# Two token tiles of the last run read the second expert table in order, by matrix products, instead of gathering its rows

## The chip, the core and the metric

The kernel runs on one core of a Trainium2 chip. Five engines have instruction streams of their own: TensorE (PE), VectorE (DVE), ScalarE (ACT), GpSimd (POOL) and SyncE (SP). They meet through semaphores. POOL issues the row gathers, SP most other transfers, and all transfers of the core run on its 16 DMA engines. The metric is the device time of one execution in microseconds (us).

## What is computed

A layer of a streaming encoder for 1024 prompt tokens and 32 sample tokens of width 1024, everything in float32. The attention branches and projections stand first. What matters here is the retrieval of single-neuron experts behind them:

```
sc = einsum("thjd,hjnd->thjn", q, subkeys)      # 8 heads, 2 halves, 128 keys
s1, i1 = top_k(sc[:, :, 0], 16);  s2, i2 = top_k(sc[:, :, 1], 16)
best, sel = top_k(s1 + s2 (all 256 pairs), 16)  # idx = i1 * 128 + i2 of those picked
g  = softmax(best)
ue = take(u, idx);  ve = take(v, idx)           # tables u, v: 16384 rows x 1024
a  = gelu(einsum("thkd,td->thk", ue, h))
y  = x + einsum("thk,thkd->td", g * a, ve)      # then a final rmsnorm
```

Each token thus picks 8 x 16 = 128 rows of `u` and the same 128 rows of `v`, 4 KB each.

## The kernel before

The tokens lie in tiles of 128 (tile 8 holds the 32 sample tokens). They are worked in three runs, (0, 1, 8), (2, 3, 4) and (5, 6, 7), and each run goes through dense stages: inputs, attend, merge, out, score. `ORDER` lists the tiles by place, so places 6, 7 and 8 are tiles 5, 6 and 7, the third run.

The expert work is a second program, woven between the dense stages. It goes in **steps** k = 0 to 1099. Sixteen steps make a group (one head of one tile). A full tile has 128 steps, place 6 begins at step 672, place 7 at 800, place 8 at 928, and the dots end with step 1055. In step k:

- POOL (`pool`) issues the gather of the `u` rows of step k (`gather_u`, 128 rows, 512 KB) and, 40 steps late (`V_LAG`), the gather of `v` rows number k - 40 (`gather_v`). Both pass through the helper `gather`, line 713. The `u` rows have one row for each token's partition, the `v` rows are sorted otherwise: one gather holds 128 picks of a few tokens.
- DVE (`experts_dve`) waits for the `u` rows and forms the dot products of 128 tokens in one instruction (line 2060). In steps 0, 2, 4, 6 and 8 of a group it also ranks the next group's scores (`rank`, `gate`), which gives the indices.
- ACT (`experts_act`) does the exponentials and the gelu, and spreads each pair of groups' weights into the matrix `zw` (`spread`).
- PE (`weigh_rows`, line 2226) takes four `v` gathers at a time, a **quad**: 8 products of 128x32 weights with 512 columns, summed in the PSUM tile `y_sum`.

At a tile's end (`tile_end`) DVE adds the residual row `x1` and normalises (`finish_sum`, `finish_norm`), and ACT stores it. POOL keeps 8 `u` and 10 `v` buffers in flight while dense stages run; 16 steps after the last dense stage's step (735) the memory of those stages is used for 5 and 4 more (`MORE_U`, `MORE_V`, class `Ring`). Step lists are fixed in the code: `plan` sets, by costs written in `ticks`, at which step each dense piece stands, and every engine follows the same weave.

Of the kernel before, what the change touches and what calls it, by code (L numbers as in the profile page):

```python
# [219 lines left out]
PIECES = [sum(64 if t == SAMPLE else 256 for t in ORDER[:at]) for at in range(TILES + 1)]  # L220


class Ring:


    def __init__(self, n, more, at, total):
        free, uses, last = list(range(n)), [0] * (n + more), [None] * (n + more)
        self.slot, self.use, self.prev = [], [], []
        for k in range(total):
            if k == at:  # L230
                free = list(range(n, n + more)) + free
            slot = free.pop(0)
            free.append(slot)
            uses[slot] += 1
            self.slot.append(slot)
            self.use.append(uses[slot])
            self.prev.append(last[slot])
            last[slot] = k
# [11 lines left out]
class Kernel:  # L250
# [8 lines left out]
    def memory(self):  # L259
# [15 lines left out]
        self.ranks = keep("ranks", [P, TOPK])  # L275
# [52 lines left out]
        with ExitStack() as ctx:  # L328
            self.u_rows += [sb(ctx, f"G_u_rows{SLOTS_U + i}", [P, D]) for i in range(MORE_U)]
            self.v_rows += [sb(ctx, f"G_v_rows{SLOTS_V + i}", [P, D]) for i in range(MORE_V)]  # L330
# [140 lines left out]

    def semaphores(self):
# [49 lines left out]
        self.u_in = [sem(f"g_u_in{i}") for i in range(SLOTS_U + MORE_U)]  # L522
        self.v_in = [sem(f"g_v_in{i}") for i in range(SLOTS_V + MORE_V)]
# [4 lines left out]
        self.y_taken, self.squares, self.roots, self.y_ready = (sem(n) for n in ("g_y_taken", "g_squares", "g_roots", "g_y_ready"))  # L528

    def counts(self):  # L530
# [16 lines left out]
        self.last_dense = self.plan()[-1] - PRELUDE + 2 * SLOTS_U  # L547
        self.ring_u = Ring(SLOTS_U, MORE_U, self.last_dense, U_SLOTS)
        self.ring_v = Ring(SLOTS_V, MORE_V, self.last_dense - V_LAG, U_SLOTS)
        self.f_out0 = sums([16 * (1 + sp.sample) * HEADS // 2 for sp in SPANS])  # L550

# [91 lines left out]
    def pool(self, pool):  # L643
# [15 lines left out]
        pool.iota(self.ranks[:, :], pattern=[[1, TOPK]], base=0, channel_multiplier=0,  # L659
# [1310 lines left out]
    def rank(self, dve, m, piece):  # L1970
# [31 lines left out]
        else:  # L2002
# [14 lines left out]
            dve.tensor_reduce(self.key[:, :, :].rearrange("p j k -> p (j k)"), hot[:, :, :], AX, ALU.add)  # L2017
            dve.drain()
            cols = slice(TOPK * (m % 2), TOPK * (m % 2 + 1))
            dve.scalar_tensor_tensor(out=self.idx[m // 2 % 2][:, cols], in0=self.key[:, 0, :], scalar=float(P), in1=self.key[:, 1, :],  # L2020
                                     op0=ALU.mult, op1=ALU.add).then_inc(self.ranked, 1)
            if m % 2:
                dve.drain()
                dve.transpose(self.idxT[m // 2 % 3][:, :], self.idx[m // 2 % 2][:, :]).then_inc(self.idx_turned, 1)
# [7 lines left out]
    def weigh(self, dve, n):  # L2032
        b = n // 2
        cols = slice(TOPK * (n % 2), TOPK * (n % 2 + 1))
        dve.wait_ge(self.gelu_done, n + 1)
        dve.tensor_tensor(self.weights[b % 2][:, cols], self.gelus[n % 2][:, :], self.gates[n % 4][:, :], ALU.mult)
        if n % 2:
            if b >= 2:
                dve.wait_ge(self.z_made, b - 1)
            dve.drain()  # L2040
            dve.transpose(self.wT[b % 2][:, :], self.weights[b % 2][:, :]).then_inc(self.w_turned, 1)

    def experts_dve(self, dve):
# [7 lines left out]
        finish = {tile_end(at) + 2: at for at in range(TILES)}  # L2051
        for k in range(STEPS):
# [22 lines left out]
            if k - 1 in finish:  # L2075
                self.finish_norm(dve, finish[k - 1])
            yield

    def finish_sum(self, dve, t):
        x1 = self.x1  # L2080
        dve.wait_ge(self.weighed, (tile_end(t) + 1 - V_LAG) // 4)
# [7 lines left out]
    def finish_norm(self, dve, t):  # L2089
        if t == 0:  # L2090
            dve.wait_ge(self.g_fin_in, 16)
        dve.wait_ge(self.roots, t + 1)
# [48 lines left out]
    def store_y(self, act, at):  # L2141
        act.wait_ge(self.y_ready, at + 1)
# [8 lines left out]
    def spread(self, act, b):  # L2151

        z, first = self.zw[b % 2], 4 if GROUP[2 * b][1] == SAMPLE else 0
# [11 lines left out]
    def experts_act(self, act):  # L2165
# [10 lines left out]
        finish = {tile_end(at) + 2: at for at in range(TILES)}  # L2176
        h2_at = {TOPK * FIRST[at] - 20: at for at in range(1, TILES)}
        x1_at = {TOPK * FIRST[at] + 58: at for at in range(TILES)}
        for k in range(STEPS):
# [4 lines left out]
            if c == 2 and n % 2 == 0 and 2 <= n <= GROUPS_ALL:  # L2184
                self.spread(act, n // 2 - 1)
# [25 lines left out]
    def weigh_rows(self, pe, quad):  # L2211
        b, i = divmod(quad, QUADS)
        at = GROUP[2 * b][0]
        first, last_of = 2 * b == FIRST[at] and i == 0, 2 * b + 2 == FIRST[at + 1] and i == QUADS - 1
        if i == 0:
            pe.wait_ge(self.z_made, b + 1)
        if first and at:
            pe.wait_ge(self.y_taken, at)
# [9 lines left out]
        last.then_inc(self.weighed, 1)  # L2228

# [6 lines left out]
def build(nc, a, outs):  # L2236
# [6 lines left out]
    with ExitStack() as ctx:  # L2243
# [8 lines left out]
        def _(sp):  # L2252
            k.weave(k.dense(k.inputs_sp, k.memory_sp, k.attend_sp, k.merge_sp, k.out_sp, k.score_sp, sp), idle(sp, STEPS + PRELUDE))

# [77 lines left out]
```

## Time and profile before

| | us |
|---|---|
| median of 3 executions | 4154.73 |
| lowest, highest | 4143.67, 4164.61 |
| span of the profiled execution | 4055.0 |
| median less span | 99.7 |
| PE, DVE, POOL busy | 2755.5, 2362.3, 2392.4 |
| moved by all transfers | 1373.95 MB, of it 1107.43 MB by the gathers' queue |

The span runs from the first to the last instruction; launch and end lie around it. A busy share over the whole span mixes the dense stages with the last quarter, in which only the expert steps are left, so the stages have to be read apart. "Granted clock" is TensorE's clock as a part of 2.4 GHz; the two levels it has are 1.2 and 2.4 GHz, and a value between is a mixture over the stretch. A wait marked "issue" is one in which the engine waited for nothing that the profile shows. A product in float32 leaves two matmul records in the trace.

### The profile page before, as it was taken

To read this page: it belongs to the slowest core of one execution; us is meant where nothing else is said; L and a number is where in the kernel's file an instruction comes from. 1 tells how busy PE (TensorE), PEld (TensorE's weight loads), DVE (VectorE), ACT (ScalarE), POOL (GpSimd) and SP (SyncE) were. 2 spreads that over 40 slices of the span, in tenths; PEclk is the share of its full clock that TensorE was granted. 3 is DMA by queue.
4 is the path that set the end of the run, shared out by engine and by line. 5 is a ranking of instruction groups with operands and counts; after the bars stand their busy time and mean duration, and the time that the engine had idled before them with its cause. 6 is when DMAs were issued, how large, how long until landed. Compare 5 with 4: busy or idle time off the path is not lost.

```text
span 4055.0 us, 39016 instructions
## 1 busy us (share of the span) xinstructions
PE 2755.5 (68%) x12071; PEld 1452.6 (36%) x12071; DVE 2362.3 (58%) x6192; ACT 853.5 (21%) x1884; POOL 2392.4 (59%) x2148
## 2 busy tenths in 40 slices
PE   8989987877789975568787888987453332333334
PEld 5667564534445432234444444443121000000000
DVE  2134356578865556646488886654566666666552
ACT  1235212244421110112144442111010000000000
POOL 1000034667756547756477776654777777777775
PEclk9989988977779987779877778998776665566556
DMA  6443387999999989989999999997999999999998
GB/s 219 124 142 101 139 285 268 389 359 385 390 349 394 386 336 375 395 312 387 356 387 361 385 394 394 381 374 289 368 391 388 381 370 367 385 387 366 382 369 345
DMA packets 540797, 1373.95 MB, mean 339 GB/s; under 512 B 50640, under 2 KB 246800, under 8 KB 540592
## 3 DMA queue, kind: packets, MB, share of 16 engines
q0 software_dynamic: 304128, 1107.43, 71.4%
q1 hardware_dynamic: 195040, 220.24, 16.2%
q10 hardware_dynamic: 41424, 43.80, 3.3%
q8 instruction: 99, 1.62, 0.2%
q14 instruction: 106, 0.87, 0.1%
HBM read 1319.26 MB, written 52.02 MB: 338 GB/s over the span
## 4 chain that ended last, share of the span: by engine, by line
PE 33%; POOL 25%; DMA 13%; DVE 11%; issue 10%; DVEq 3%; ACT 2%; SPq 1%; ACTq 1%; PEldq 0%; POOLq 0%; PEld 0%
POOL G_v_rows L713 13%; POOL G_u_rows L713 12%; PE scores L837 7%; DMA G_v_rows<-in_peer_v,G_idxT 5%; PE scores L1721 5%; PE y_sum L2226 4%; PE scores L1725 3%; DVE G_u_rows L2060 3%; PE scores L1915 3%; PE scores L1503 3%; PE scores L1810 2%; DMA scratch_dkT<-A_dkT 2%; PE scores L1410 2%; PE o L1445 1%; DMA D_w_br<-in_w_br_m 1%
## 5 line engine op out<-in xcount | busy, mean ns | idle before, releaser
L713 POOL DMA_INDIRECT G_u_rows<-in_peer_u,G_idx x1056 | 1199.9, 1136 | 756.7 <-issue 321.8
L2060 DVE CUSTOM_DVE_ANT_0 G_u_rows<-G_u_rows,G_h 128x1024 f32<-128x1024 f32 x1056 | 1274.7, 1221 | 431.2 <-DMA G_u_rows<-in_peer_u,G_idx 408.4
L713 POOL DMA_INDIRECT G_v_rows<-in_peer_v,G_idxT x1056 | 1177.9, 1115 | 486.9 <-issue 312.4
L2226 PE MATMUL y_sum<-G_v_rows,G_zw 128*32 128x512 f32 x4224 | 749.7, 846 | 877.1 <-DMA G_v_rows<-in_peer_v,G_idxT 853.0
L2226 PEld LDWEIGHTS y_sum<-G_v_rows,G_zw 128*32 128x32 f32 x4224 | 148.9, 137 | 1358.5 <-issue 1354.6
L837 PE MATMUL scores<-A_w_in,A_hT 128*128 128x256 f32 (+2 forms) x864 | 221.9, 417 | 22.9 <-DMA A_w_in<-in_w_in 15.5
L668 POOL MEMSET G_zw<- 128x1024 f32 x2 | 1.9, 963 | 395.9 <-SPq L630 395.9
L837 PEld LDWEIGHTS scores<-A_w_in,A_hT 128*128 128x128 f32 x864 | 168.7, 198 | 74.8 <-DMA A_w_in<-in_w_in 16.4
L1721 PE MATMUL scores<-D_hT,D_w_gate 128*128 128x384 f32 x512 | 172.9, 491 | 2.3 <-DMA D_w_br<-in_w_br_m 2.1
L1428 PE MATMUL turn<-ident,C_probs 128*128 128x128 f32 x635 | 133.4, 327 | 49.1 <-ACT C_pT L1536 41.2
L1960 DVE COPY F_sc<-scores 128x256 f32<-128x256 f32 (+1 forms) x72 | 29.3, 422 | 215.2 <-PE scores L1926 215.1
L1523 ACT ACTIVATE C_probs<-C_probs,C_ntop 128x128 f32<-128x128 f32 (+5 forms) x144 | 104.8, 729 | 187.3 <-DVEq L1597 182.2
L2183 ACT ACTIVATE G_gelus<-G_dots 128x16 f32<-128x16 f32 x66 | 14.2, 216 | 602.6 <-DVEq L2064 602.3
L1428 PEld LDWEIGHTS turn<-ident,C_probs 128*128 128x128 f32 x635 | 87.8, 170 | 144.7 <-ACT C_pT L1536 75.0
L837 PE MATMUL scores<-A_hT,A_w_in 128*128 128x384 f32 x384 | 132.4, 499 | 9.7 <-issue 9.7
L1410 PE MATMUL scores<-C_k_diff,C_q_diff 32*128 32x512 f32 (+4 forms) x416 | 108.5, 631 | 44.3 <-DVE C_ntop L1594 36.9
L1915 PE MATMUL scores<-h2T,F_w_q 128*128 128x384 f32 (+1 forms) x384 | 126.7, 489 | 17.1 <-DMA F_skT<-scratch_skT 17.1
L1599 DVE TENSOR_REDUCE C_ntop<-scores 128x1 f32<-128x256 f32 (+8 forms) x108 | 65.9, 610 | 121.3 <-PE scores L1410 120.3
L1536 ACT ACTIVATE C_pT<-turn 128x512 f32<-128x512 f32 (+3 forms) x216 | 102.7, 475 | 135.8 <-PE turn L1428 135.0
L1410 PE MATMUL scores<-C_k_mla,C_q_mla 104*128 104x512 f32 (+4 forms) x208 | 97.8, 588 | 42.3 <-SPq L630 36.3
L1721 PEld LDWEIGHTS scores<-D_hT,D_w_gate 128*128 128x128 f32 x512 | 95.3, 190 | 83.8 <-issue 17.6
L1915 PE MATMUL scores<-h2T,DF_w 128*128 128x384 f32 (+1 forms) x384 | 124.6, 483 | 1.0 <-issue 0.6
(282 smaller groups left out, 3940.7 us busy)
## 6 DMA issues: line engine op xcount, KB each, us to landing
A_w_in<-in_w_in SPq DMA_DIRECT2D x24, 1024.0 KB, 13.3
D_w_gate<-in_w_gate SPq DMA_DIRECT2D x24, 1024.0 KB, 22.9
G_u_rows<-in_peer_u,G_idx POOLq DMA_INDIRECT x1056, 7.8
G_v_rows<-in_peer_v,G_idxT POOLq DMA_INDIRECT x1056, 8.2
DF_w<-in_w_gate SPq DMA_DIRECT2D x12, 1024.0 KB, 21.0
DF_w<-in_peer_wq SPq DMA_DIRECT2D x12, 1024.0 KB, 10.3
F_w_q<-in_peer_wq SPq DMA_DIRECT2D x12, 1024.0 KB, 7.1
E_w_o<-in_w_o SPq DMA_DIRECT2D x18, 512.0 KB, 8.5
```

What stands on the lines that cost most here:

```text
L713: pool.indirect_dma_start(out=buf[:, :], out_offset=None, in_=table, in_offset=bass.IndirectOffsetOnAxis(ap=rows, axis=0)).then_inc(signal ...
L837: last = pe.matmul(self.ps_m[n % 4][:, 0:width], lhs[c], rhs[c], start=(c == 0), stop=(c == len(lhs) - 1))
L1410: last = pe.matmul(self.ps_s[(slot + k) % 2][:, c:c + n], lhs, rhs, start=True, stop=True)
L1428: last = pe.transpose(ps_t[at % banks][0:w, b - c:b - c + P], probs[:, b:b + w], ident[:, :])
L1503: last = pe.matmul(self.ps_m[1 + 2 * (unit % 2)][:, 0:sp.n], self.D[0]["w_gate"][b][:, c, par * P:(par + 1) * P], hT[:, c, 0:sp.n], start= ...
L1523: act.activation(probs[:, 0:keys], src[:, 0:keys], ACT.Exp, bias=m["ntop"][:, col:col + 1], scale=-1.0 if kind == "diff" else 1.0, accum_o ...
L1536: last = act.activation(m["pT"][j % 2][:, c:c + full], src[:, 0:full], ACT.Copy)
L1721: pe.matmul(gates[:, 0:n], m["w_gate"][b][:, c, block], m["hT"][:, c, :], start=(c == 0), stop=(c == DC - 1))
L1725: last = pe.matmul(branch[:, 0:n], m["w_br"][b][:, c, block], m["oT"][:, 4 * b + c, :], start=(c == 0), stop=(c == 3))
L1915: last = pe.matmul(self.ps_m[k % 2][:, 0:n], w[:, c, j * P:(j + 1) * P], m["h2T"][:, c, :], start=(c == 0), stop=(c == DC - 1))
L2060: dve.tensor_tensor_reduce(out=self.u_rows[slot][:, :], in0=self.u_rows[slot][:, :], in1=self.h2[t % 2][:, :], scale=1.0, scalar=0.0, op0= ...
L2226: last = pe.matmul(self.ps_y[32 * c:32 * (c + 1), cols], self.zw[b % 2][:, lo:lo + 32], self.v_rows[self.ring_v.slot[4 * quad + c]][:, col ...
```

## The change

Places 6 and 7 (`STREAMED`) keep their `u` gathers and dots. Their 256 `v` gathers and 64 quads go. In their place:

1. `rank` and `weigh` leave the two key numbers and the weights of all 128 picks of each token of such a tile in `keys_of` and `weights_of`. A tick "turn" transposes them with three PE transposes and an ACT copy (`picksT`), so that picks lie on partitions.
2. A tick "build" makes, for 8 tokens and one half (64) of the first key, two one-hot arrays on DVE (128x512 and 128x1024 elements, and a 128x512 multiplication by the weight), 8 small PE products (128x128 by 64 columns) and one ACT copy of 128x512 into `spread_w`: the weight matrix from table rows to tokens. There are 2 tiles x 2 halves x 16 = 64 builds.
3. A tick "chunk" reads 128 rows of `v` in table order. SP loads two chunks (1 MB) at a time into one of two buffers (`stream_sp`), a buffer being loaded again when PE is done with its two chunks. For each of 128 chunks PE makes 4 products of 128x128 weights with 512 columns, two for each tile, summed in the PSUM tiles `scores`.
4. "sum" and "norm" add `x1` and normalise both tiles at the end; SP loads their `x1` and stores them.

`spread_w` holds one half of the keys, so the second half's builds stand behind chunk 63. The extra buffers `MORE_U` and `MORE_V` go, their memory being used by the new arrays. The list of ticks, by `stream_at`, is: step 802 turn of place 6; 803 to 921 its first 16 builds; 930 turn of place 7; 931 to 961 its 16 builds; 963 to 1012 chunks 0 to 63; 1013 to 1037 the other 32 builds; 1038 to 1087 chunks 64 to 127; 1090 to 1095 sums and norms.

```diff
-SLOTS_U, SLOTS_V, MORE_U, MORE_V = 8, 10, 5, 4
+SLOTS_U, SLOTS_V = 8, 10
+STREAMED = (6, 7)
+HALVES, CHUNKS, TOGETHER, CHUNK_SLOTS = 2, P, 8, 2
+KEYS_HALF = P // HALVES
+LAST_CHUNK = 1088
...
-            if k == self.last_dense:
-                pool.wait_ge(self.opened, len(STAGES) + 1)
             if k < U_SLOTS:
                 self.gather_u(pool, k)
-            if k >= V_LAG:
-                self.gather_v(pool, k - V_LAG)
+            if k >= V_LAG and by_row(k - V_LAG):
+                self.gather_v(pool, v_of(k - V_LAG))
...
-            if v >= 0 and v % 4 == 3 and v < U_SLOTS:
-                self.weigh_rows(pe, v // 4)
+            if v >= 0 and v % 4 == 3 and v < U_SLOTS and by_row(v):
+                self.weigh_rows(pe, v)
+            for tick in self.stream.get(k - 1, ()):
+                self.stream_pe(pe, *tick)
...
+    def stream_sp(self, eng):
+        for c in range(0, CHUNKS, 2):
+            slot = c // 2 % CHUNK_SLOTS
+            if c >= 2 * CHUNK_SLOTS:
+                eng.wait_ge(self.t_streamed, c - 2 * CHUNK_SLOTS + 2)
+            rows = self.a["peer_v"][P * c:P * (c + 2), :].rearrange("(c p) n -> p c n", p=P)
+            eng.dma_start(self.chunks[slot][:, :, :], rows).then_inc(self.t_in[slot], 16)
...
+    def stream_dve(self, dve, kind, *at):
...
+            if u >= 2:
+                dve.wait_ge(self.t_turned, self.turn_no[self.builds[u - 2]] + 1)
...
+            dve.tensor_tensor(first, self.count[:, lo:lo + KEYS_HALF].unsqueeze(1).to_broadcast([P, TOGETHER, KEYS_HALF]),
+                              each(0, KEYS_HALF), ALU.is_equal)
+            dve.tensor_tensor(second, self.count[:, :].unsqueeze(1).to_broadcast([P, TOGETHER, P]), each(1, P), ALU.is_equal)
+            dve.drain()
+            last = dve.tensor_tensor(first, first, each(2, KEYS_HALF), ALU.mult)
...
+    def stream_pe(self, pe, kind, *at):
...
+            if i == 0:
+                pe.wait_ge(self.t_turn_out, self.built[half])
+            if c % 2 == 0:
+                pe.wait_ge(self.t_in[slot], 16 * (c // (2 * CHUNK_SLOTS) + 1))
+            for s in range(len(STREAMED)):
+                for cols in (slice(0, D // 2), slice(D // 2, D)):
+                    last = pe.matmul(self.ps_s[s][:, cols], self.spread_w[:, i, P * s:P * (s + 1)], self.chunks[slot][:, c % 2, cols],
+                                     start=(c == 0), stop=(c == CHUNKS - 1))
+            last.then_inc(self.t_streamed, 1)
...
+    def stream_act(self, act, kind, *at):
...
+            if half and g == 0:
+                act.wait_ge(self.t_streamed, KEYS_HALF * half)
```

How the order on the engines moves, at the three places that matter. First POOL, at the gathers around step 712; before, the two kinds alternate to the end:

```order
L713 DMA G_u_rows<-in_peer_u,G_idx 128x1024
L713 DMA G_v_rows<-in_peer_v,G_idxT 128x1024
L713 DMA G_u_rows<-in_peer_u,G_idx 128x1024
L713 DMA G_v_rows<-in_peer_v,G_idxT 128x1024
L713 DMA G_u_rows<-in_peer_u,G_idx 128x1024
```

and in the changed program at the same place:

```order
L765 DMA G_u_rows<-in_peer_u,G_idx 128x1024
L765 DMA G_v_rows<-in_peer_v,G_idxT 128x1024
L765 DMA G_u_rows<-in_peer_u,G_idx 128x1024 x257
L765 DMA G_v_rows<-in_peer_v,G_idxT 128x1024
L765 DMA G_u_rows<-in_peer_u,G_idx 128x1024
```

For 257 gathers POOL issues `u` rows alone; then the pairs of place 8 begin. Second PE, from its last dense products (`DF_w`, `F_w_q` are score weights) on; before, the quads of the last three tiles are mixed in and follow:

```order
L1915 MATMUL scores<-h2T,DF_w 128x384 x8
L1926 MATMUL scores<-DF_w_br,F_qT_0 128x128 x6
L2226 MATMUL y_sum<-G_v_rows,G_zw 32x512 x16
L1915 MATMUL scores<-h2T,F_w_q_1 128x384 x8
L2226 MATMUL y_sum<-G_v_rows,G_zw 32x512 x8
L1915 MATMUL scores<-h2T,F_w_q_1 128x384 x8
L1926 MATMUL scores<-F_skT_1,F_qT_1 128x128 x6
```

In the changed program the turn and the builds (`T_hot`) stand there instead, up to the first chunk products:

```order
L1967 MATMUL scores<-h2T,F_w_q_1 128x384 x16
L1978 MATMUL scores<-F_skT_1,F_qT_1 128x128 x6
L2376 MATMUL turn<-ident,g_q 128x128 x2
L2376 MATMUL turn<-ident,g_kv 128x128
L2382 MATMUL o<-T_hot_0 128x64 x8
L2382 MATMUL turn<-T_hot_1 128x64 x8
...
L2395 MATMUL scores<-T_chunks,T_spread_w 128x512 x36
L2298 MATMUL y_sum<-G_v_rows,G_zw 32x512 x8
L2395 MATMUL scores<-T_chunks,T_spread_w 128x512 x24
L2298 MATMUL y_sum<-G_v_rows,G_zw 32x512 x8
```

Each quad of place 8 now stands behind some 20 chunk products. Third, PE between chunk 63 and chunk 64, where no product of the stream stood before:

```order
L2298 MATMUL y_sum<-G_v_rows,G_zw 32x512 x8
L2395 MATMUL scores<-T_chunks,T_spread_w 128x512 x12
L2382 MATMUL turn<-T_hot_0 128x64 x8
L2382 MATMUL o<-T_hot_1 128x64 x8
L2298 MATMUL y_sum<-G_v_rows,G_zw 32x512 x8
L2382 MATMUL turn<-T_hot_0 128x64 x8
```

The second half's 32 builds are an island between the two halves of the stream.

## Rows read from the trace of the kernel before

**Rows 1.** The page: span, and busy tenths in 40 slices of 101 us

```profile
span 4055.0 us, 39016 instructions
PE   8989987877789975568787888987453332333334
DVE  2134356578865556646488886654566666666552
PEclk9989988977779987779877778998776665566556
DMA  6443387999999989989999999997999999999998
```

**Rows 2.** Busy time by stretch; first line names the columns, from, to, length ahead

```profile
core 0: us, PE busy (x) PEld busy (x) DVE busy (x) ACT busy (x) POOL busy (x), PEclk, DMA share, GB/s
2500.00:2700.00 200.00, 189.03 (x716) 98.57 (x715) 118.13 (x285) 34.98 (x54) 127.56 (x115) 0.99 1.03 386
3000.00:3100.00 100.00, 54.44 (x248) 24.24 (x252) 64.06 (x158) 12.46 (x22) 75.67 (x71) 0.77 1.03 392
3100.00:3988.00 888.00, 282.40 (x1264) 53.68 (x1256) 554.87 (x1364) 71.02 (x134) 697.11 (x627) 0.58 1.00 377
4000.00:4055.00 55.00, 25.49 (x144) 5.11 (x136) 3.97 (x5) 0.20 (x1) 25.31 (x27) 0.67 0.78 300
```

**Rows 3.** Waits from 3100 to 3988 us: total, times, longest

```profile
PE y_sum L2226 <- DMA G_v_rows<-in_peer_v,G_idxT: 606.4, 79, 10.6
DVE G_u_rows L2060 <- DMA G_u_rows<-in_peer_u,G_idx: 308.4, 233, 3.8
```

**Rows 4.** Line 2060 (the dots) from 3000 to 3100 us, and its wait

```profile
L2060 DVE CUSTOM_DVE_ANT_0 G_u_rows<-G_u_rows,G_h x33: 1183/1224/1280, 3000.0 to 3098.7; 128x1024 f32<-128x1024 f32 x33
...
  DMA G_u_rows<-in_peer_u,G_idx: 14.6, 10
```

**Rows 5.** DVE's groups from 3100 to 3988 us: count, busy us, mean ns, idle before

```profile
L2060 DVE CUSTOM_DVE_ANT_0 G_u_rows<-G_u_rows,G_h 128x1024 f32<-128x1024 f32 x316 | 386.3, 1225 | 311.2 <-DMA G_u_rows<-in_peer_u,G_idx 308.4 <-issue 2.7
...
L2010 DVE TENSOR_TENSOR G_work<-ranks,G_partf 128x512 f32<-128x512 f32 x19 | 13.2, 693 | 1.4
...
L2083 DVE TENSOR_TENSOR G_x<-y_sum,G_x 128x1024 f32<-128x1024 f32 x2 | 2.4, 1218 | 0.0
```

**Rows 6.** Line 713 (the gathers) from 3100 to 3988 us: ns min/median/max, landing

```profile
L713 POOL DMA_INDIRECT G_v_rows<-in_peer_v,G_idxT x316: 933/992/1991, 3099.6 to 3987.7; - x158
L713 POOL DMA_INDIRECT G_u_rows<-in_peer_u,G_idx x311: 933/940/1985, 3101.0 to 3981.1; - x156
...
DMA to landing us min/median/max: 5.3/6.6/13.2
```

**Rows 7.** Groups from 2723 to 2785 us: products of the out stage, 512 columns

```profile
L1810 PE MATMUL scores<-E_w_o,mergedT 128*128 128x512 f32 x72 | 31.5, 594 | 1.7 <-DMA E_w_o<-in_w_o 1.7
```

**Rows 8.** Line 2226 (quads): 2500 to 2700, then 3200 to 3800 us, then the last quad

```profile
L2226 PE MATMUL y_sum<-G_v_rows,G_zw x224: 589/592/617, 2505.8 to 2694.1; 128*32 128x512 f32 x112
...
L2226 PE MATMUL y_sum<-G_v_rows,G_zw x832: 623/1061/1063, 3206.7 to 3791.1; 128*32 128x512 f32 x167
...
4041.00 1.92 PE L2226 MATMUL y_sum<-G_v_rows,G_zw 128*32 128x512 f32 x16 [1.27 <-DMA G_v_rows<-in_peer_v,G_idxT]
```

**Rows 9.** Loads by SP of 1 MB, 2700 to 3100 us; by ACT of 512 KB, from 3100

```profile
L1901 SPq DMA_DIRECT2D F_w_q<-in_peer_wq x4: 372/372/383, 2797.7 to 3013.2; - x4
...
DMA to landing us min/median/max: 5.6/10.7/15.3
...
G_h<-scratch_h ACTq DMA_DIRECT2D x2, 512.0 KB, 7.6
```

**Rows 10.** Groups of the page: ACT copy of 128x512 out of PSUM

```profile
L1536 ACT ACTIVATE C_pT<-turn 128x512 f32<-128x512 f32 (+3 forms) x216 | 102.7, 475 | 135.8 <-PE turn L1428 135.0
```

**Rows 11.** The end, in order of time: start, length, what

```profile
4042.98 1.23 DVE L2083 TENSOR_TENSOR G_x<-y_sum,G_x 128x1024 f32<-128x1024 f32 x1 [53.06 <-PE y_sum L2226]
...
4047.50 5.55 ACTq L2145 DMA_DIRECT2D out_y<-G_x  x16
```

More of the change, by code:

```diff
@@ L219, with by_row, v_of, __init__ @@
 H2_LOADED = [sum(64 if t == SAMPLE else 16 for t in ORDER[at % 2:at + 1:2]) for at in range(TILES)]
-PIECES = [sum(64 if t == SAMPLE else 256 for t in ORDER[:at]) for at in range(TILES + 1)]
-class Ring:
[L226 to L238, printed above, removed]
+PIECES = [sum(0 if a in STREAMED else 64 if t == SAMPLE else 256 for a, t in enumerate(ORDER[:at])) for at in range(TILES + 1)]
+SUMMED = [sum(a not in STREAMED for a in range(at)) for at in range(TILES + 1)]
+PASSED = (TOPK * FIRST[STREAMED[0]], TOPK * FIRST[STREAMED[-1] + 1])
+V_SLOTS = U_SLOTS - (PASSED[1] - PASSED[0])
+def by_row(step):
+    return not PASSED[0] <= step < PASSED[1]
+def v_of(step):
+    return step - max(0, min(step, PASSED[1]) - PASSED[0])
+class Ring:
+    def __init__(self, n, total):
+        self.slot = [k % n for k in range(total)]
+        self.use = [k // n + 1 for k in range(total)]
+        self.prev = [k - n if k >= n else None for k in range(total)]
 def span_of(t):
@@ L328, in memory @@
         with ExitStack() as ctx:
[L329 to L330 removed]
+            self.stream_memory(ctx, sb)
         def psum(name, cols):
@@ L2050, in experts_dve @@
         yield
-        finish = {tile_end(at) + 2: at for at in range(TILES)}
+        finish = {tile_end(at) + 2: at for at in range(TILES) if at not in STREAMED}
         for k in range(STEPS):
@@ L2076, in experts_dve @@
                 self.finish_norm(dve, finish[k - 1])
+            for tick in self.stream.get(k, ()):
+                self.stream_dve(dve, *tick)
             yield
@@ L2206, in experts_pe, with weigh_rows @@
             v = k - V_LAG
-            if v >= 0 and v % 4 == 3 and v < U_SLOTS:
-                self.weigh_rows(pe, v // 4)
+            if v >= 0 and v % 4 == 3 and v < U_SLOTS and by_row(v):
+                self.weigh_rows(pe, v)
+            for tick in self.stream.get(k - 1, ()):
+                self.stream_pe(pe, *tick)
             yield
-    def weigh_rows(self, pe, quad):
+    def weigh_rows(self, pe, step):
+        at, quad = GROUP[step // TOPK][0], v_of(step) // 4
         b, i = divmod(quad, QUADS)
-        at = GROUP[2 * b][0]
-        first, last_of = 2 * b == FIRST[at] and i == 0, 2 * b + 2 == FIRST[at + 1] and i == QUADS - 1
+        first, last_of = step == TOPK * FIRST[at] + 3, step == TOPK * FIRST[at + 1] - 1
         if i == 0:
@@ new lines, in stream_dve, with each @@
+    def stream_dve(self, dve, kind, *at):
+        tick = (kind,) + at
+        if kind == "build":
+            s, half, g = at
+            u = self.build_no[tick]
+            if u == 0:
+                dve.wait_ge(self.opened, len(STAGES) + 1)
+            if half == 0 and g == 0:
+                dve.wait_ge(self.t_turn_out, self.turn_no["turn", s] + 1)
+            if u >= 2:
+                dve.wait_ge(self.t_turned, self.turn_no[self.builds[u - 2]] + 1)
+            picks, lo = self.picksT[s], KEYS_HALF * half
+            toks = slice(TOGETHER * g, TOGETHER * (g + 1))
+            first, second = self.hot1[u % 2][:, :, :], self.hot2[u % 2][:, :, :]
+            def each(j, n):
+                return picks[:, j, toks].unsqueeze(2).to_broadcast([P, TOGETHER, n])
+            dve.tensor_tensor(first, self.count[:, lo:lo + KEYS_HALF].unsqueeze(1).to_broadcast([P, TOGETHER, KEYS_HALF]),
[3 more added lines that the diff above has]
+            last = dve.tensor_tensor(first, first, each(2, KEYS_HALF), ALU.mult)
+            last.then_inc(self.t_hot, 1)
+        elif kind == "sum":
+            s, = at
+            x1, y = self.chunks[0][:, s, :], self.ps_s[s]
+            if s == 0:
+                dve.wait_ge(self.t_streamed, CHUNKS)
+                dve.wait_ge(self.t_in[0], 16 * (CHUNKS // 4 + len(STREAMED)))
+            dve.tensor_tensor(x1, y[:, :], x1, ALU.add)
+            dve.drain()
+            dve.tensor_tensor_reduce(out=y[:, :], in0=x1, in1=x1, scale=1.0 / D, scalar=EPS,
+                                     op0=ALU.mult, op1=ALU.add, accum_out=self.t_ms[:, s:s + 1])
+            dve.drain().then_inc(self.t_finish, 1)
+        elif kind == "norm":
+            s, = at
+            x1 = self.chunks[0][:, s, :]
+            dve.wait_ge(self.t_finish, 3 * s + 2)
+            dve.reciprocal(self.t_rs[:, s:s + 1], self.t_root[:, s:s + 1])
+            dve.drain()
+            dve.scalar_tensor_tensor(out=x1, in0=x1, scalar=self.t_rs[:, s:s + 1], in1=self.g_fin[:, :],
+                                     op0=ALU.mult, op1=ALU.mult).then_inc(self.t_finish, 1)
```

153 lines of the change are left out of this document (130 added, 23 removed).

## The prediction, made before the changed kernel was run

> **What bounds the kernel now.** I read the page's slices first [rows 1]: from about slice 6 the DMA row stands at 9 almost without a break, and from slice 30 PE is at 3 and DVE at 6. So the last quarter is paced by transfers. The stretch table says the same with numbers [rows 2]: from 3100 to 3988 us the transfer engines are busy at a share of 1.00 and move 377 GB/s. The waits say who suffers [rows 3]: DVE waits 308.4 us for `u` rows, PE 606.4 us for `v` rows. 316 dots lie in those 888 us [rows 5], so a step takes 888/316 = 2.81 us, in which two gathers of 512 KB go. Since the dots end with step 1055, the first of these is step 740. From 3000 to 3100 us 33 dots passed [rows 4], so step 712 lies near 3015 us and step 963 near 3101 + 223 x 2.81 = 3728 us. From there to the end of the span are 327 us.
>
> **What goes.** 256 `v` gathers of 512 KB, 134 MB, are replaced by 67 MB in order. At 377 GB/s [rows 2] the 67 MB saved are worth 178 us, but only where transfers stay the bound. So I follow the steps in three stretches and ask in each which engine ends last.
>
> **Steps 712 to 739** (dense score stage, 85 us before). Gone are the `v` gathers and 7 quads. DVE waited there 14.6 us in 33 steps for `u` rows [rows 4], so 12 us in 28; PE was at 54 of 100 us [rows 2]. Gain between 0 and 30 us; I take 15, near the wait.
>
> **Steps 740 to 962**, with `u` gathers alone. POOL can issue a gather each 0.94 us plus 0.30 of issue [rows 6], the transfer engines one each 524288 B/377 GB/s = 1.39 us. DVE is slower than both: what is left of its step when the wait is taken out is (888 - 308.4)/316 = 1.83 us [rows 3, 5]. It becomes the bound, 223 x (2.81 - 1.83) = 219 us gained. The smaller number of buffers costs nothing here: 8 steps of 1.83 us are 14.6 us against 6.6 from issue to landing [rows 6]. But 32 builds lie here, on DVE. A build is one instruction of 512 elements at 693 ns, one of 1024 at about 1218 and a second of 512 [rows 5]: 2.6, with gaps 2.7 us; 32 make 86 us. Their 8 PE products of 64 columns and an ACT copy of 0.48 us [rows 10] run beside. Net gain 133, together with the first stretch 148 us; step 963 comes at 3580 instead of 3728 us. Bounds 100 (gathers stretched by DVE) to 165.
>
> **Steps 963 to the end: the new critical work.** All 128 chunks stand behind step 963. A product of 128x128 weights with 512 columns left two records, and 72 records took 31.5 us at full clock [rows 7]: 0.875 us for a product. A chunk has 4, so 3.5 us; 128 chunks are 448 us of PE alone, already more than the 327 us that were left. This is the term that decides, and nothing hides it: the chunks can't begin before both tiles' weights are known. The quads of place 8 stand between them, 0.39 for each pair of chunks, at 1.9 us [rows 8], 0.75 us for a pair. PE needs at least 7.75 us for a pair, 64 pairs are 496 us.
>
> Whether PE is kept busy hangs on two buffers. The load for pair p + 2 starts when pair p is done and must land while PE works on p + 1. The trace has no load of 1 MB in rows of 4 KB, so I bound it. Below: 1 MB score weights landed in 5.6 us at least. Above: 15.3 at most; the median was 10.7 [rows 9]. A load of half the size, in 4 KB rows as here, took 7.6 beside the gathers [rows 9], and 512 KB more at 377 GB/s are 1.4: 9.0. Transfers will have some room (per pair 1 MB and 3.1 gathers, 2.7 MB in 9 us, 300 GB/s), so I take 9.5, and 1.0 for SP's wait and issue. Two pairs then take 10.5 + 7.75 = 18.2 us, a pair 9.1, and 64 of them 582 us. PE's gaps stay near 1.4 us a pair. From 2500 to 2700 us PE was busy 189 of 200 us with a clock of 0.99; in the tail, where it waits up to 10.6 us for a quad's rows, it has 0.58 and a quad's records take 1061 instead of 592 ns [rows 2, 3, 8]. I therefore take 2.4 GHz for the chunks.
>
> Between the halves lie steps 1013 to 1037. DVE can make two builds ahead, then waits for PE, so 24 steps x 1.83 + 30 builds x 2.7 = 125 us pass with the stream standing; meanwhile the gathers go on. At the end SP must still load two `x1` tiles (behind chunk 126), and DVE adds and normalises three tiles instead of one. Before, the last quad to the end took 14 us, store included [rows 8, 11]; I take 30, from 22 to 40. DVE's `u` dots of these steps hide behind PE (9.1 us for 1.56 steps).
>
> Sum: 582 + 125 + 30 = 737 us instead of 327, a loss of 410. Less 148 gained: +262 us. Against the profiled execution's own span, 4055 + 262 = 4317; with the 99.7 us that lie around it, 4417 us, or 4415. The change halves the bytes and then loses more than twice the gain by serial PE work in the last quarter.
>
> **A rule of the notes on landing.** The Trainium skill, DMA: Bandwidth & Descriptors, "Anatomy of one DMA", gives a fit of about 2.0 us plus bytes over 436 GB/s; as an estimate, 4.4 us for 1 MB, and by it the loads would be hidden and the sum would be the first rival's. The rows do not agree under load: 512 KB took 7.6 us there.
>
> **The rivals.**
>
> *Loads hidden, PE alone the bound.* If a load lands within 6.75 us (plus the 1.0), a pair takes 7.75 us: 496 instead of 582 us, 86 less: 4331 us. For it: the shortest landing of 5.6, and that transfers have room. Against: medians of 10.7 and 7.6. Chance 0.24.
>
> *Slow loads.* At 15.3 + 1.0 us a pair takes 12.0, 770 us in all: 188 more, 4605 us. If the gaps become so long that the clock falls to 1.2 GHz, PE is at 100% with 15 us for a pair, which is the same kind of case and worse; but then it has no gaps, which speaks against a lasting fall. Chance 0.14 for times above 4500.
>
> *POOL takes DVE's place in steps 740 to 962.* Gathers took 0.93 to 1.99 us [rows 6]. If DVE's denser work stretched each to 1.99, with 0.30 a step would take 2.29 instead of 1.83 us: 103 us more, 4520 us. The mean row is near its minimum with DVE busy at 62%, which speaks against it. The Trainium skill, SBUF — State Buffer, "SBUF: two separate sides", has a mechanism for such a case: VectorE instructions with two SBUF inputs (dots and builds are such) and GpSimd lock each other out of a shared port for a whole instruction. Chance 0.05.
>
> *Faster.* If the stream kept the pace of the transfers, 178 us would be saved: 3977 us. It decides at the pair: gains win only if the 64 pairs take less than 327 + 148 - 155 = 320 us, 5.0 us for a pair, so a product below about 0.55 us. All 96 records of the out stage speak against it. Chance 0.03.
>
> **How the numbers follow.** Forecast 4415 us (4370 to 4500) 0.52, hidden loads 0.24, slow loads 0.14, POOL 0.05, faster 0.03, and 0.02 that the sums cancel. The range has to take in PE alone with all of the gain (4331 - 17 - 8 for a short end, so 4305) and a landing up to the longest one (4600). This kernel's measurement can tell about 0.5% (21 us) from no change. Slower by more: 0.95; faster by more: 0.03; within: 0.02.
>
> **What would show it.** In the changed profile: steps 740 to 962 with DVE busy nearly without a wait for `u` rows, transfers well below 1.00 and 1.8 to 1.9 us a dot; then PE at 8 to 9 tenths with a clock of 0.9 or more, two stretches of about 290 us, with a valley of 125 us between in which DVE is full; chunk products at 0.44 us a record; PE waiting for `T_chunks` by 1 to 2 us for a pair. I am wrong if the DVE step stays above 2.3 us, if PE's clock in the stream is below 0.8, if the valley is not there, or if a pair takes less than 7 or more than 12 us.

## The result, and the profile of the changed kernel

The changed kernel took 4328.5 us (median of 4 executions, 4316.8 to 4355.2) where the kernel before took 4151.0 (4143.7 to 4164.6): ratio 1.0425, 95% interval 1.0383 to 1.0467. It is slower by 177 us. The prediction said slower, with 4415 us and a range of 4305 to 4600. The measured time lies in that range, but outside its centre of 4370 to 4500, which held a chance of 0.52.

The page of the changed kernel, in 40 slices of 108 us, to be read against [rows 1]:

```profile
span 4315.0 us, 41005 instructions
PE   8989978777799755687677789855402237888897
DVE  2133266487755456565788856545799997228301
PEclk9999989877699877798877889977755557997899
DMA  6343569999999899999999999889887767776665
```

Before, the last quarter was one plateau: DMA at 9, DVE at 6, PE at 3. Now it has three parts. From slice 29 to 32 (counted from 0) DVE is at 9, PE at 0 to 3 and its clock at 5. From slice 33 on PE stands at 7 to 9 and DMA at 5 to 7. In slice 36 DVE comes back to 8 and the clock drops to 7. The stretch table has steps 740 to 962 in its first row (two dots at its edges left out); the others are cut by the first and last chunk products of the two halves (columns as in [rows 2]):

```profile
3126.00:3602.00 476.00, 116.13 (x508) 110.47 (x509) 453.64 (x1069) 77.53 (x106) 298.36 (x226) 0.50 0.76 258
3605.00:3894.00 289.00, 260.57 (x690) 105.91 (x690) 97.17 (x242) 12.66 (x23) 104.39 (x103) 0.94 0.80 297
3894.00:4021.00 127.00, 106.88 (x625) 85.77 (x623) 114.34 (x188) 39.38 (x43) 52.55 (x48) 0.68 0.67 228
4021.00:4294.00 273.00, 253.78 (x712) 102.58 (x712) 16.91 (x31) 2.48 (x6) 57.50 (x59) 0.98 0.65 233
4294.00:4315.00 21.00, 3.50 (x32) 0.79 (x26) 11.68 (x15) 0.61 (x3) 0.00 (x0) 0.71 0.24 75
```

The transfer engines, at 1.00 before [rows 2], are at 0.65 to 0.80 up to the last chunk product. The bytes fell from 1374 to 1307 MB, but transfers are no longer what ends last. Line 2125 (the dots, line 2060 before) from 3126 to 3602 us, DVE's group with its idle time, and POOL's gathers from 3100 to 3500 us:

```profile
L2125 DVE CUSTOM_DVE_ANT_0 G_u_rows<-G_u_rows,G_h 128x1024 f32<-128x1024 f32 x222 | 263.1, 1220 | 4.4 <-issue 4.4
...
L2339 DVE TENSOR_TENSOR T_hot<-count,T_picksT 128x1024 f32<-128x1024 f32 x32 | 39.0, 1218 | 0.0
L2341 DVE TENSOR_TENSOR T_hot<-T_hot,T_picksT 128x512 f32<-128x512 f32 x32 | 22.2, 693 | 2.4
...
L765 POOL DMA_INDIRECT G_u_rows<-in_peer_u,G_idx x201 | 268.6, 1336 | 134.0 <-DVE G_dots L2125 86.1 <-issue 47.9
```

DVE's wait for `u` rows, 308.4 us in [rows 5], is gone altogether in these steps, and POOL now waits for DVE. Steps 740 to 962 with their 32 builds take 478 us (3124.8 to 3603.3); 223 x 1.83 + 86 = 494 was forecast. Less the 86 us of the builds, a step is 1.76 us. The gathers do get longer beside the denser DVE work, 1336 ns on average against 1112 before (697.11 us for 627, [rows 2]), but with 0.3 of issue they take 1.64 us, still a little less than DVE's step. The Trainium skill, SBUF — State Buffer, "SBUF: two separate sides", names such a mutual lock of VectorE and GpSimd; the longer gathers agree with it, and no run here isolates it.

Line 2395 (chunk products) in the two halves of the stream, with what it waited for (us, times; PE's own waits and those of its weight loads are added up there), and the group of the second half alone with PE's own wait behind the bar:

```profile
L2395 PE MATMUL scores<-T_chunks,T_spread_w x512: 592/592/1222, 3605.5 to 3893.5; 128*128 128x512 f32 x171
...
  DMA T_chunks<-in_peer_v: 66.0, 24
...
L2395 PE MATMUL scores<-T_chunks,T_spread_w x512: 592/592/1222, 4021.3 to 4293.3; 128*128 128x512 f32 x171
...
  DMA T_chunks<-in_peer_v: 47.8, 23
...
L2395 PE MATMUL scores<-T_chunks,T_spread_w 128*128 128x512 f32 x512 | 232.0, 610 | 19.2 <-DMA T_chunks<-in_peer_v 19.2
```

The last record takes 0.6 us, so the halves last 289 and 273 us, 9.0 and 8.5 us for a pair of chunks. PE itself stood 27.9 us in the first half and 19.2 us in the second for `T_chunks`, 0.9 and 0.6 us for a pair. Between them are 127 us without a chunk product. TensorE, busy for 116 of the 476 us ahead of the stream, had there its lower level, 1.2 GHz (0.50), and 0.94 and 0.98 of 2.4 GHz in the stream.

**One thing about the times.** The kernel before took 4144 to 4176 us on two occasions and 4060 to 4082 us on three others, below called the slower and the quicker level, and the trace in [rows 1 to 11] belongs to the quicker one.

### The profile page after: what moved, and what is told of

Same layout as the page of the kernel before. It is cut to its first block, busy times and chain, and to the rows that moved or that the text cites. A ratio compares the mean times of both kernels' runs of the same rounds, so it can differ in the third digit from the quotient of the medians.

```text
span 4315.0 us, 41005 instructions
## 1 busy us (share of the span) xinstructions
PE 3161.7 (73%) x13101; PEld 1797.1 (42%) x13101; DVE 2498.6 (58%) x6368; ACT 913.3 (21%) x1916; POOL 2151.3 (50%) x1892
## 4 chain that ended last, share of the span: by engine, by line
PE 41%; DVE 23%; DMA 11%; issue 11%; DVEq 5%; POOL 3%; ACT 3%; another core or an unknown queue 2%; SPq 1%; ACTq 0%; PEldq 0%; PEld 0%; POOLq 0%
DVE G_u_rows L2125 9%; PE scores L2395 7%; PE scores L889 7%; PE scores L1773 5%; DMA T_chunks<-in_peer_v 5%; PE y_sum L2298 4%; PE scores L1777 4%; PE scores L1967 3%; PE scores L1555 2%; PE scores L1462 2%; POOL G_u_rows L765 2%; POOL G_v_rows L765 2%; DMA scratch_dkT<-A_dkT 2%; DMA G_v_rows<-in_peer_v,G_idxT 1%
## 5 line engine op out<-in xcount | busy, mean ns | idle before, releaser
L765 POOL DMA_INDIRECT G_u_rows<-in_peer_u,G_idx x1056 | 1254.5, 1188 | 925.9 <-DVE G_dots L2125 496.7
L765 POOL DMA_INDIRECT G_v_rows<-in_peer_v,G_idxT x800 | 882.1, 1103 | 811.5 <-PE y_sum L2298 553.4
L2298 PE MATMUL y_sum<-G_v_rows,G_zw 128*32 128x512 f32 x3200 | 486.8, 738 | 199.2 <-DMA G_v_rows<-in_peer_v,G_idxT 168.7
L2395 PE MATMUL scores<-T_chunks,T_spread_w 128*128 128x512 f32 x1024 | 473.0, 619 | 48.3 <-DMA T_chunks<-in_peer_v 47.1
L2395 PEld LDWEIGHTS scores<-T_chunks,T_spread_w 128*128 128x128 f32 x1024 | 198.5, 198 | 323.3 <-issue 255.3
L2298 PEld LDWEIGHTS y_sum<-G_v_rows,G_zw 128*32 128x32 f32 x3200 | 98.8, 126 | 458.5 <-issue 454.3
L2382 PE MATMUL turn<-T_hot 128*128 128x64 f32 x512 | 102.3, 383 | 151.4 <-DVE T_hot L2341 149.1
L2382 PE MATMUL o<-T_hot 128*128 128x64 f32 x512 | 101.0, 380 | 112.2 <-DVE T_hot L2341 109.8
L2382 PEld LDWEIGHTS turn<-T_hot 128*128 128x128 f32 x512 | 97.8, 293 | 159.5 <-issue 147.8
L2382 PEld LDWEIGHTS o<-T_hot 128*128 128x128 f32 x512 | 96.4, 290 | 120.5 <-issue 106.4
```

The source lines that it names most:

```text
L765: pool.indirect_dma_start(out=buf[:, :], out_offset=None, in_=table, in_offset=bass.IndirectOffsetOnAxis(ap=rows, axis=0)).then_inc(signal ...
L2298: last = pe.matmul(self.ps_y[32 * c:32 * (c + 1), cols], self.zw[b % 2][:, lo:lo + 32], self.v_rows[self.ring_v.slot[4 * quad + c]][:, col ...
L2382: last = pe.matmul(bank[:, KEYS_HALF * i:KEYS_HALF * (i + 1)], self.hot2[u % 2][:, i, :], self.hot1[u % 2][:, i, :], start=True, stop=True)
L2395: last = pe.matmul(self.ps_s[s][:, cols], self.spread_w[:, i, P * s:P * (s + 1)], self.chunks[slot][:, c % 2, cols], start=(c == 0), stop= ...
```

## The experiments

The eight runs of this table fell on two occasions of the quicker level, so they can also be set against each other. The first four are of one execution each, and on their occasion the kernel before, executed twice, took 4059.9 and 4070.5 us: from these two, by estimate, a difference of less than 15 us says nothing there. `nochunk`, `noisland` and `halfprod` leave out work that the outputs need.

| kernel | time, us | span of its profile | kernel before there | ratio, 95% interval |
|---|---|---|---|---|
| before_again | 4059.9 | 4058.1 | 4070.5 | |
| nochunk | 3905.2 | 3903.4 | 4070.5 | |
| noisland | 4143.3 | 4141.5 | 4070.5 | |
| halfprod | 4177.0 | 4175.2 | 4070.5 | |
| after_again (the change) | 4274.2 | 4272.6 | 4070.8 | 1.0486, 1.0465 to 1.0507 |
| single | 4195.1 | 4197.0 | 4070.8 | 1.0299, 1.0281 to 1.0316 |
| early | 4049.4 | 4042.9 | 4070.8 | 0.9943, 0.9927 to 0.9960 |
| early_single | 4046.1 | 4040.1 | 4070.8 | 0.9939, 0.9922 to 0.9956 |

### Where the time between span and median lies

`before_again` is the kernel before without an edit.

> The kernel before, unchanged, to find where the 96 us between the profiled execution (span 4055) and the median of its timed executions (4151) lie. Theory A: the profiled execution was an unusually quick one, little lies around the span (of the changed kernel's profiled execution it was 4316.8 against a span of 4315.0), and other executions have a longer span because the stretches that are paced by transfers run slower: span about 4145, 2.9 to 3.0 us instead of 2.81 for a step after 3100 us, fewer than 377 GB/s there. Theory B: about 97 us of each execution of the kernel before lie outside its span: span about 4055 with a time of about 4150.

Its execution took 4059.9 us with a span of 4058.1: 1.8 us lie around a span, not 97. Theory B has fallen. Theory A holds in its first half, that the profiled execution was a quick one; this run was quick as well, so it doesn't show a slower execution of the kernel before, and no trace of one is kept. `after_again` is the changed kernel beside the kernel before, again on an occasion of the quicker level.

> The changed kernel, unchanged, beside the kernel before on one chip. The kernel before took 4144 to 4165 us where it was timed first, but 4060 and 4070 us on another chip, where it had 381 GB/s after 3100 us. Theory: the stretches paced by gathers follow the chip, the stream (PE and landing) does not, so on a chip where the kernel before takes about 4065 us the changed one takes about 4275 (3561 to the first chunk product, 562 for the stream, 127 for the island, 21 at the end), ratio 1.05; on one where it takes 4150 about 4325, ratio 1.04. Rival (the ratio is the same on both): 1.0425 again, 4238 us on the quicker chip.

Measured 4274.2 us and 1.0486, against 4275 and 1.05 expected; the rival's 4238 us is out, and its constant ratio of 1.0425 too, though the two intervals (up to 1.0467 there, from 1.0465 here) just touch. Its trace against the changed kernel's first one shows where the 42 us between their spans are. First the line of the stream's start in this run, then the stretch from 2000 to 2500 us, of the first profile of the changed kernel and of this one, where both run code that the change did not touch:

```profile
L2395 PE MATMUL scores<-T_chunks,T_spread_w x512: 592/592/1222, 3561.4 to 3848.0; 128*128 128x512 f32 x171
```

```profile
2000.00:2500.00 500.00, 364.71 (x2023) 204.30 (x2023) 391.98 (x972) 200.76 (x423) 345.05 (x305) 0.79 0.97 364
```

```profile
2000.00:2500.00 500.00, 394.48 (x2111) 222.36 (x2112) 405.99 (x1030) 206.37 (x433) 362.44 (x318) 0.79 0.99 377
```

The first chunk product stands at 3605.5 in one and 3561.4 in the other, 44 us apart; from there to the end both take the same, 709.5 and 711.2 us. All of the 44 us lie ahead of step 740, which starts at 3124.8 and 3081.0 us: steps 740 to 962, paced by DVE, take 478 us in both. The slower level moves 364 instead of 377 GB/s in the stretch shown. So the level acts on stretches that transfers pace. The changed kernel has fewer of them and is touched less: its median is 54 us higher on the slower level, that of the kernel before 80 us.

### The gain side alone

`nochunk` leaves out 124 of 128 chunks, loads and products; the builds stay.

```diff
-        rest = [("chunk", c) for c in range(KEYS_HALF)]
+        rest = [("chunk", c) for c in range(4)]
...
-        rest += [("chunk", c) for c in range(KEYS_HALF, CHUNKS)]
...
-        for c in range(0, CHUNKS, 2):
+        for c in range(0, 4, 2):
```

> The changed kernel with 124 of the 128 chunks left out, their loads and their products; the v rows of the two tiles aren't gathered, all 64 builds remain (the second 32 spread from step 976 to 1084). The outputs of tiles 5 and 6 lack most of their expert sum. This is the gain side alone. My theory (the loss is the stream's own PE time and the island of builds): without them the end comes some 330 to 345 us after step 963 as before, so a span of 3602 + 340 = about 3940, 210 below the kernel before. Rival (the gathers go slower because of the smaller number of buffers, or DVE's builds cost more than their time): 4050 or more.

Its stretch table, up to the first chunk product and from there to the end:

```profile
3100.00:3560.00 460.00, 118.57 (x519) 112.72 (x519) 438.43 (x1038) 76.72 (x104) 289.95 (x219) 0.50 0.77 255
3560.00:3903.00 343.00, 208.32 (x1056) 112.03 (x1056) 238.79 (x474) 54.43 (x74) 251.73 (x210) 0.65 0.91 334
```

From the first chunk product (3559.9 us) to the end are 343 us, in the expected 330 to 345. The span is 155 us below `before_again` (165 below the other execution of the kernel before on that occasion); the text said 210 against the slower level's 4151. The first chunk product stands 172 us ahead of step 963 of `before_again` (3731.7 us), and 17 us of that are lost again behind it, where the kernel before needed 326 us. A cost of the smaller number of buffers, of the size that the rival wanted, does not show.

### The island

`noisland` leaves the second half's builds out, so chunk 64 follows chunk 63.

```diff
-        rest += [("build", s, 1, g) for s in range(len(STREAMED)) for g in range(units)]
```

> The changed kernel without the second half's 32 builds: chunk 64 follows chunk 63, with the first half's weights again (so the outputs of tiles 5 and 6 are others). Theory: the 127 us between the last product of chunk 63 and the first of chunk 64 are DVE time in which the stream stands, so the span falls by 115 to 127 us to about 4190 to 4200. Rival (the valley serves the gathers, which otherwise would pace the stream): the pairs of chunks become slower than 9.0 and 8.5 us and less than 70 us are saved.

Line 2394 (its chunk products) over the whole run, then the stretch table from its first to its last:

```profile
L2394 PE MATMUL scores<-T_chunks,T_spread_w x1024: 592/592/1223, 3561.2 to 4120.1; 128*128 128x512 f32 x171
...
3561.00:4120.00 559.00, 521.15 (x1503) 209.54 (x1504) 153.01 (x363) 20.53 (x40) 215.73 (x210) 0.97 0.86 319
```

131 us less than `after_again`, whose island is 127 us long, and the stream still takes 560 us, 8.75 a pair. The island costs all of its length, within the 15 us that single executions can tell: the gathers that ran in it find room beside the stream (transfer share 0.86). The rival is out. (4190 in the text was meant for the slower level; 4272.6 - 131 is the same statement.)

### What paces a pair of chunks

`halfprod` leaves out the right half of the columns for chunks 1 to 126.

```diff
-                for cols in (slice(0, D // 2), slice(D // 2, D)):
+                for cols in (slice(0, D // 2), slice(D // 2, D))[:2 if c == 0 or c == CHUNKS - 1 else 1]:
```

> The changed kernel with 2 instead of 4 products a chunk (the right half of the columns is left out for chunks 1 to 126, so half the columns of tiles 5 and 6 lack their expert sum); loads, builds and gathers as they are. A pair of chunks took 9.0 and 8.5 us. Theory (a load of about 9.7 us and PE's own time alternate with two buffers): PE's part of a pair falls from 7.75 to 4.25 us, a pair takes (9.7 + 4.25)/2 = 7.0 us, 64 pairs 448 instead of 562 us, span about 4200. Rival 1 (PE alone): 4.25 us a pair, span about 4025. Rival 2 (loads alone): a pair stays at 8.5 to 9, span above 4280.

Line 2395 in the two halves of its stream, with the wait for chunks:

```profile
L2395 PE MATMUL scores<-T_chunks,T_spread_w x260: 592/592/1222, 3558.8 to 3793.6; 128*128 128x512 f32 x130
...
  DMA T_chunks<-in_peer_v: 149.9, 37
...
L2395 PE MATMUL scores<-T_chunks,T_spread_w x260: 592/592/1222, 3926.6 to 4153.5; 128*128 128x512 f32 x130
...
  DMA T_chunks<-in_peer_v: 139.3, 35
```

The halves take 235.4 and 227.5 us, 7.4 and 7.1 for a pair, with 7.0 expected; rival 1 wanted 4.25, rival 2 8.5 or more. With 3.5 us less of products a pair got only 1.5 to 1.6 shorter; two alternating terms would give half of 3.5. One caution: in the first half the transfer share was 0.94, so part of the 7.4 may be the transfers' own pace.

`single` cuts the same memory into four buffers of one chunk.

```diff
-        for c in range(0, CHUNKS, 2):
-            slot = c // 2 % CHUNK_SLOTS
+        for c in range(CHUNKS):
+            slot = c % (2 * CHUNK_SLOTS)
             if c >= 2 * CHUNK_SLOTS:
-                eng.wait_ge(self.t_streamed, c - 2 * CHUNK_SLOTS + 2)
...
+                eng.wait_ge(self.t_streamed, c - 2 * CHUNK_SLOTS + 1)
```

> The changed kernel with the same 2 MB of chunk memory cut into four buffers of one chunk instead of two of two: a load is issued after each chunk and has three chunks (10.5 us and more) to land. Theory (a pair took 9.0 and 8.5 us because load and products alternate): the loads hide, a pair takes PE's own 7.75 us, 64 pairs 496 instead of 562 us, so 50 to 66 us less than the changed kernel, ratio to it 0.985 to 0.988. Rival (the transfer engines, with gathers and stream together, pace the pairs): no difference over 15 us.

The stretch table for the two halves of its stream, and PE's group of chunk products with its waits:

```profile
3557.00:3801.00 244.00, 244.00 (x691) 101.83 (x692) 97.16 (x242) 12.06 (x22) 109.43 (x103) 0.99 0.94 353
3931.00:4176.00 245.00, 245.00 (x708) 101.39 (x712) 16.40 (x31) 2.48 (x6) 58.19 (x59) 1.00 0.75 259
...
L2395 PE MATMUL scores<-T_chunks,T_spread_w 128*128 128x512 f32 x1024 | 448.2, 597 | 1.1 <-ACT T_spread_w L2415 1.1
```

PE is busy for the whole of both halves at a clock of 0.99 and 1.00 and never waits for `T_chunks`: the loads hide, and a pair takes 7.65 us, against 7.75 expected. The time fell by 79 us, more than the 50 to 66 expected, since a pair had stood at 9.0 and 8.6 and PE's own time is a little shorter. The rival (transfers pace the pairs) is out. The edit changes two things at once, the size of a load (512 KB) and how far ahead it is issued (three chunks); which of them does more was not tried. What is left, 490 us of products and quads at full clock, is the floor of this placement.

### The stream earlier

`early` changes one line, so that the stream takes places 5 and 6 and runs over 250 steps from step 835; `early_single` adds the four buffers.

```diff
-STREAMED = (6, 7)
+STREAMED = (5, 6)
```

> STREAMED = (5, 6) instead of (6, 7): the stream takes the tiles of places 5 and 6 (tiles 4 and 5), whose weights are ready at step 802, so the chunks begin at step 835 instead of 963 and have 250 instead of 125 steps; a step has 0.5 chunks, 1.8 us of PE, beside 1.3 MB of transfers, 3.5 us at 377 GB/s. Theory (the loss comes from serial PE work behind step 963, not from the stream as such): PE is no longer the bound, the island's builds find 50 steps, and the time falls by at least 150 us against the changed kernel, to about the kernel before (within 60 us of it). By the rows: 270 us for steps 735 to 835, 774 us of transfers to step 1088, 25 at the end, 1070 in place of the 970 us of the kernel before, and up to 100 less for the dense stages in steps 584 to 735, that lose their v gathers. Rival (one-hot builds and products cost what they cost wherever they stand): within 60 us of the changed kernel.

> Both edits: places 5 and 6 streamed, four buffers of one chunk. Theory: with the earlier place the stream is paced by transfers, so the finer buffers add less than 20 us to the gain of the place alone. Rival (landing of the loads still stands in the way): 40 us or more less than with the place alone.

The stretch table of `early`, from the first chunk product to the last:

```profile
3203.00:3500.00 297.00, 259.08 (x798) 99.00 (x799) 158.00 (x394) 20.92 (x38) 195.84 (x179) 0.94 1.02 408
3500.00:3700.00 200.00, 153.70 (x763) 98.50 (x762) 179.02 (x364) 45.71 (x58) 149.21 (x117) 0.70 0.95 353
3700.00:3926.00 226.00, 199.80 (x656) 80.71 (x656) 118.46 (x272) 16.23 (x28) 152.94 (x136) 0.93 1.01 404
3926.00:4021.00 95.00, 91.73 (x315) 35.12 (x313) 1.49 (x4) 2.49 (x6) 31.83 (x34) 1.00 0.90 330
```

225 us less than the changed kernel, and 0.6% less than the kernel before, clear of the interval but small. The products, builds and loads are the same and only stand beside transfers now, so the rival has fallen. The transfer engines are back at 0.90 to 1.02, and the finer buffers add 3 us, inside the spread. The gain is small beside the 178 us that the saved bytes are worth. The table gives a likely reason, which no run isolates: from 3500 to 3700 the builds hold DVE at 179 of 200 us and the transfer rate falls to 353, and the stretch before the stream has DVE as its bound too (from 3000 to 3100 us 95.5 of 100 us, at 226 GB/s).

The last four runs asked whether PE's work behind the last dot (busy 92 of 95 us from 3926 to 4021) is on the path. `LAST_CHUNK` says at which step the last chunk stands.

```diff
-LAST_CHUNK = 1088
+LAST_CHUNK = 1064
```

> Places 5 and 6 streamed, four buffers of one chunk, and LAST_CHUNK = 1064 instead of 1088: the same chunks closer together, so that the last ones and the final additions of both tiles stand beside the last gathers. With 1088, PE was busy 97 of 100 us from 3900 to 4000 us and the last chunk product came 20 us before the end, with the dots done at 3926. Theory: behind the dots PE has 32 steps of 1.8 us of chunk products and quads on top, longer than the 41 v gathers (1.24 us each); moving 24 steps' share of them forward, where transfers are the bound, takes 15 to 30 us off: 4015 to 4030 on the chip where it took 4046. Rival (the transfers that the chunks bring are the bound everywhere): within 10 us of 4046.

> The same with LAST_CHUNK = 1036. By the theory the gain is used up once PE's work behind the dots is shorter than the last gathers; a step then has 0.64 chunks beside it, 1.38 MB of transfers, still above PE's 2.6 us, but the 32 builds of the island stand in 40 instead of 45 steps, where DVE is the bound: no better than with 1064, 4015 to 4040. Rival: the island costs more, above 4046.

These two fell on the slower level: 4101.3 and 4107.7 us against 4163.5, ratios 0.9848 (0.9820 to 0.9876) and 0.9865 (0.9838 to 0.9891). Between 1064 and 1036 that shows no difference outside the intervals, and it says nothing on 1088, so 1088 and 1064 were run side by side.

> LAST_CHUNK = 1088 once more, beside the next kernel on the same chip, since the kernel before takes 4071 us on one chip and 4164 on another and the two values of LAST_CHUNK were measured on different ones. Theory (PE's work behind the dots is on the path with 1088): 15 to 30 us above the next kernel. Rival: within 10 us of it.

> LAST_CHUNK = 1064, with the kernel above on one chip: 15 to 30 us below it by the theory, within 10 us by the rival.

4044.9 against 4043.6 us (ratios to the kernel before 0.9937 and 0.9936). My theory has fallen. First the stretch behind the dots with 1088, then with 1064:

```profile
3926.00:4021.00 95.00, 93.77 (x331) 35.64 (x330) 3.21 (x6) 2.49 (x6) 31.82 (x34) 1.00 0.91 333
```

```profile
3926.00:4021.00 95.00, 72.25 (x292) 25.22 (x294) 19.53 (x32) 2.89 (x8) 46.51 (x46) 0.91 0.98 383
```

PE got its room, but the transfers now fill the stretch (share 0.98 against 0.91). The work moved forward delayed the gathers there: the last dot ends at 3957 us instead of 3927. The place is bounded from both sides.

The version that beats both kernels is thus `early_single`: 0.994 of the kernel before on occasions of the quicker level (three measurements with and without the last edit, 0.9936 to 0.9939), and with `LAST_CHUNK` 1064 0.985 on one of the slower.

## Why the prediction was right, and where it was off

The sum by its own terms, for spans:

| term | predicted | first profile | after_again |
|---|---|---|---|
| first chunk product at | 3580 | 3605 | 3561 |
| 64 pairs | 582 | 561 | 563 |
| island | 125 | 127 | 127 |
| end | 30 | 21 | 21 |
| span | 4317 | 4315 | 4273 |

**Steps 712 to 962** (gain 148 us). Right in cause: DVE's wait is gone. Counted by dots, steps 712 to 739 take 77.5 us in `before_again` and 58.2 in `after_again`, a gain of 19 where 15 was taken; steps 740 to 962 take 622.5 and 478.2 us, a gain of 144 where 133 was forecast, because DVE's step was 1.76 and not 1.83 us. Step 712 itself stands 9 us earlier, which no edit explains.

**The stream** (582 us). Right in mechanism: two buffers that let landing and products alternate (shown by `single` and `halfprod`), 0.453 us a record in the second half (232.0 us for 512) against 0.4375, a clock of 0.94 and 0.98. Landing and SP's share together were put at 10.5 us; 2 x 9.0 - 7.65 gives 10.4 in the first half and 2 x 8.5 - 7.65 gives 9.4 in the second, with the slower records counted in. From issue to landing alone the loads of `after_again` took 8.5 us in the first half and 6.8 in the second (medians), where 9.5 was taken; over the whole run:

```profile
DMA to landing us min/median/max: 2.6/7.3/13.7
```

The fit in the Trainium skill, DMA: Bandwidth & Descriptors, "Anatomy of one DMA", as an estimate 4.4 us for 1 MB, does not agree with that median. The section gives the fit for transfers that GpSimd issues, while these are issued by SP, which the prediction didn't say; the measurement decides. The rival of hidden loads was nearer than a chance of 0.24 suggests: the same memory in four buffers made it true.

**The island** (125 us): right to 2 us, and `noisland` shows that all of it is on the path. **The end**: 21 instead of 30 us, since the `x1` loads hid behind the last chunk.

**What was off** (4415, in the sum 4417, against 4328.5) lies half in the sum and half behind it. The sum gave a span of 4317, and the changed kernel on the quicker level, to which the base of 4055 belongs, had 4272.6: 44 us too high, of which 19 are the gain, 19 the stream and 9 the end, with the island 2 the other way. The other 44 us are a step that looked like bookkeeping: "with the 99.7 us that lie around it". Nothing like it lies around a span; 1.8 us do. The 99.7 us were mostly the difference of two levels, read from the kernel before, which has more stretches paced by transfers. For the changed kernel only 56 us stand between 4272.6 and the median of 4328.5: 42 between its two profiled spans, 12 from the profiled execution to the median of its occasion, and the 1.8.

That the spans 4317 and 4315 agree to 2 us is luck: terms 44 us too high, and a result of the slower level, 42 us higher. And 4328 falls on the 4331 us of the rival with hidden loads, whose mechanism was not there: a pair took 9.0 and 8.5 us, not 7.75.

Within one occasion of the quicker level the change costs 203 us by medians (4274.2 - 4070.8), and 214 by the profiled spans (4272.6 - 4058.1); on the slower level it costs 177. The forecast of 262 was too much on both.

Of the rivals, slow loads and POOL in DVE's place did not come (1.34 + 0.30 us for a gather against a step of 1.76 us), nor did the faster one: its condition, a pair in 5.0 us, is missed even by `single`. But its idea, a stream at the pace of the transfers, is what `early` does by position.

## What to carry to other kernels

Bytes saved are worth their time only where transfers end last; ask in each stretch which engine comes next once they don't (here DVE at 1.76 instead of 2.81 us a step, then PE at 7.65 us a pair and more). Work put in place of transfers has to stand beside the other transfers: with the stream behind step 963 the kernel lost 203 us, and with the stream from step 835 on it gained 0.6%. Before adding a difference of median and span to a forecast, look for an execution whose time and span are both known.

## What the hardware showed that I had not expected

Gathers alone moved 377 GB/s at a transfer share of 1.00 [rows 2], and 381 in the same stretch of `before_again`. With the table stream beside them the same engines moved more, as two rows of the stretch table of `early_last1064_b` show (last column):

```profile
3203.00:3500.00 297.00, 263.07 (x805) 102.74 (x806) 158.31 (x394) 20.50 (x37) 192.94 (x174) 0.94 1.02 409
...
3700.00:3926.00 226.00, 202.35 (x651) 79.13 (x651) 108.37 (x256) 13.03 (x25) 142.30 (x136) 0.97 1.03 414
```

409 to 414 GB/s is 7 to 10% above gathers alone, of which 2 to 3% lie in the share (1.02 and 1.03). Where weights were loaded beside gathers, the kernel before had 386 and 392 GB/s at a share of 1.03 [rows 2]. Whether it is the order of the rows or the second queue was not tried.

And executions of one kernel on different occasions differ by 1 to 2%, with the transfer rate, while within an occasion they agree to 1%. The texts on record put this down to the chip. The chip's number in the results does not bear that out: it is 8 both where the kernel before took 4071 us and where it took 4164. The cause stays open.
